# Earlier split of block 2's start, one run of matmuls for each neighbourhood row, and moved transpositions in the sticks and the sliding window

## The reference

```python
def second_block(x, ln_g, w_in, b_in, ...):
    hn = rms_norm(h, ln_g[l])
    proj = hn @ w_in[l] + b_in[l]
    glu_a, glu_b, z_conv, q, k, v, z_att = jnp.split(proj, cuts, axis=-1)
    y_conv = conformer_conv(glu_a, glu_b, dw_w[l], ...)
    y_att = neighbourhood_attention(q, k, v, rpb[l])
    ...
    h = h + y @ w_out[l]

def neighbourhood_attention(q, k, v, rpb):     # tokens as a grid with rows of 64
    def one_row(args):                         # each query row sees 8 key rows, 16 columns of each
        s = jnp.einsum("bhwd,bhiwjd->bhwij", q_row, k_win) * scale + bias
        p = jax.nn.softmax(s.reshape(B, N_HEADS, GRID_W, kh * KW), axis=-1)
        return jnp.einsum("bhwij,bhiwjd->bhwd", p, v_win)
```

## Time and profile before

| | |
|---|---|
| median of 3 runs | 2934.9 us (2932.89 to 2935.36) |
| the profiled execution, its own time | 2932.91 us |
| its span, first to last instruction | 2931.6 us |
| mean granted TensorE clock | 0.993 |
| TensorE busy | 2852.8 us (97%) |
| VectorE busy | 1929.8 us (66%) |
| ScalarE busy | 1306.0 us (45%) |

### The profile page before, as it was taken

One profiled execution on the slowest core, in us unless ns is written; L12 is line 12 of the kernel. 1 busy time (PEld: TensorE's weight loads), 2 busy tenths in 40 slices (PEclk: granted clock), 3 DMA queues, 4 the chain that ended last, 5 costly groups with the idle time before them and its releaser, 6 DMA issues.

```text
span 2931.6 us, 35692 instructions
## 1 busy us (share of the span) xinstructions
PE 2852.8 (97%) x14306; PEld 2222.7 (76%) x14306; DVE 1929.8 (66%) x2891; ACT 1306.0 (45%) x2069; POOL 13.3 (0%) x15
## 2 busy tenths in 40 slices
PE   8999999999999998999999999999899999999998
PEld 7887787788888886777775777666577788888886
DVE  5453439777777768776775685776767755555575
ACT  4223525434444346454545645556644433233335
POOL 0000000000000000000000000000000000000001
PEclk9999999999999999999999999999999999999999
DMA  4211111111111111111110110000001112111112
GB/s 161 78 57 40 40 51 37 52 49 58 44 58 58 44 58 51 37 36 37 36 36 22 43 51 22 23 23 30 30 30 51 44 43 65 51 47 55 58 51 79
DMA packets 49986, 141.73 MB, mean 48 GB/s; under 512 B 12918, under 2 KB 16798, under 8 KB 49694
## 3 DMA queue, kind: packets, MB, share of 16 engines
q1 hardware_dynamic: 49822, 139.45, 15.0%
HBM read 135.16 MB, written 9.77 MB: 49 GB/s over the span
## 4 chain that ended last, share of the span: by engine, by line
PE 80%; DVE 10%; ACT 5%; issue 4%; DMA 0%; POOL 0%; DVEq 0%; SPq 0%; ACTq 0%; POOLq 0%
PE psum L992 24%; PE psum L612 13%; PE psum L1070 13%; PE psum L1257 12%; PE psum L754 2%; PE psum L645 2%; PE psum L1382 1%; PE psum L1409 1%; PE psum L728 1%; PE psum L1198 1%; PE psum L685 1%; PE psum L1177 1%; PE psum L802 1%; DVE y L3247 1%; DVE mlp_ta L2930 1%
## 5 line engine op out<-in xcount | busy, mean ns | idle before, releaser
L2508 ACT ACTIVATE w_hi<-w_raw 128x512 fp32r<-128x512 f32 x280 | 175.1, 625 | 319.9 <-DVE w_raw L3831 190.8
L3105 DVE TENSOR_TENSOR residual<-residual,psum 128x1024 f32<-128x1024 f32 x160 | 194.3, 1220 | 122.5 <-PE psum L1070 122.4
L992 PE MATMUL psum<-h_hi,w_hi 128*128 128x512 f32 x640 | 249.1, 389 | 0.1
L992 PE MATMUL psum<-h_hi,w_lo 128*128 128x512 f32 x640 | 249.0, 389 | 0.0
L992 PE MATMUL psum<-h_lo,w_hi 128*128 128x512 f32 x640 | 249.0, 389 | 0.0
L3862 DVE TENSOR_TENSOR w_lo<-w_raw,w_hi 128x512 fp32r<-128x512 f32 x280 | 192.1, 686 | 36.0 <-ACT w_hi L2508 35.8
L612 PE MATMUL psum<-h_hi,w_hi 128*128 128x512 f32 x656 | 210.1, 401 | 4.1 <-DVE w_lo L2589 4.1
L1257 PE MATMUL psum<-h_hi,w_lo 128*128 128x512 f32 x608 | 209.9, 411 | 0.0
L1257 PE MATMUL psum<-h_hi,w_hi 128*128 128x512 f32 x608 | 206.8, 421 | 2.4 <-ACT cln_rstd L1481 1.4
L1070 PE MATMUL psum<-mlp_act_hi,w_hi 128*128 128x512 f32 x640 | 198.7, 392 | 6.1 <-DVE residual L3105 4.1
L612 PE MATMUL psum<-h_hi,w_lo 128*128 128x512 f32 x656 | 202.4, 390 | 0.0
(11 more groups left out here) (480 smaller groups left out, 5656.3 us busy)
## 6 DMA issues: line engine op xcount, KB each, us to landing
w_raw<-in_weights SPq DMA_DIRECT2D x228, 512.0 KB, 3.6
residual<-in_x_t SPq DMA_DIRECT2D x8, 512.0 KB, 8.5
out_t<-residual SPq DMA_DIRECT2D x16, 256.0 KB, 2.1
rel_copies<-rel_rows SPq DMA_DIRECT2D x8, 480.0 KB, 6.1
na_bias<-rel_copies SPq DMA_DIRECT2D x8, 240.0 KB, 4.5
band_copies<-band_rows SPq DMA_DIRECT2D x8, 192.0 KB, 6.0
ret_rotary<-in_rotary SPq DMA_DIRECT2D x1, 1024.0 KB, 12.0
swa_bias<-band_copies SPq DMA_DIRECT2D x4, 256.0 KB, 4.2
```

Source lines behind the costliest of these rows:

```text
L992: ins = self.pe.matmul(out[bank[j]], w[:, k, :], x(k), start=(j in emptied and k == 0 and part == 0), stop=(k == 3 and part == 2), skip_gr ...
L2508: ins = self.act.activation(dst, src, ACT.Copy)
L3105: self.dve.tensor_tensor(x, x, self.m.place["down", t, n], ALU.add).then_inc(*self.to("dve_down", t, n))
```

## The change

- **Block 2's start.** The squares of half 1 get places of their own in the idle tensor `y`, and VectorE's adds for that half go. TensorE makes their sum itself: `n4_squares` issues one fp32 matmul for each of the eight tiles, into the same bank, five ahead of the first projection and three at its tile (2, 0), where one stood. ScalarE makes the split of the first weight tile a square earlier, the root of half 0 two squares earlier, and the split of the second tile behind square 6 instead of behind all squares.
- **Neighbourhood.** The two runs of 9 are one of 18 (4 instead of 2 and 2 at the end); then come the products and then the turning. The orders of ScalarE and VectorE stay.
- **Sticks.** The run of 2 between scores and the first turning goes, and the run behind that turning is 6 instead of 4.
- **Sliding window.** The turning stands directly behind the scores, and one run of 8, 10 or 3 behind it.

```diff
     def n4_square(self, k, half):
+        if half:
+            return self.y[:, k // 2, k % 2 * HALF:k % 2 * HALF + HALF]
         return self.block_square(self.m_acc, (self.m_buf0, self.m_buf1), k, half)
...
+    def n4_squares(self, *tiles):
+        m = self.m
+        for k in tiles:
+            if k == 0:
+                self.n4_sum = self.take(("pe_n4_mean", 1), 5, 1, ("act_n4_rstd_ln", 1))
+            self.q.wait_ge(*self.on("act_n4_sq", k, 1))
+            ins = self.pe.matmul(self.n4_sum, m.c("mean1024"), m.n4_square(k, 1), start=(k == 0), stop=(k == KD - 1),
+                                 skip_group_check=True)
+        if tiles[-1] == KD - 1:
+            ins.then_inc(*self.to("pe_n4_mean", 1))
...
+        self.n4_squares(0, 1, 2, 3, 4)
         self.project_pair_halves(lambda k, half: ("act_n4_hi", k, half), lambda k, half: ("dve_n4_lo", k, half),
-                                 ("act_nq", 0), ("act_nv", 0), {(2, 0): lambda: self.n4_mean(1)})
+                                 ("act_nq", 0), ("act_nv", 0), {(2, 0): lambda: self.n4_squares(5, 6, 7)})
...
             if step < rows and r % 2 == 0:
                 self.na_scores(step)
-            self.run(rest, some)
+            self.run(rest, 2 * some)
             if p == PAIRS - 1 and 12 <= r < 16:
                 self.cln_square(r - 12)
+            if step >= 2:
+                self.na_out(step - 2)
             if 1 <= step <= rows:
                 self.na_turn(step - 1)
-            self.run(rest, some)
-            if step >= 2:
-                self.na_out(step - 2)
...
             self.stick_scores(d)
-            self.run(rest, 2)
             if d:
                 self.stick_turn(2 * d - 2)
-            self.run(rest, 4)
+            self.run(rest, 6)
...
-            filling = 4 if step < 6 else 5 if step < AHEAD else 3
-            if step != MEAN:
-                self.run(rest, filling)
             if TURN <= step < PAIRS * NCH + TURN:
                 self.window_turn(step - TURN)
-            if step < AHEAD:
-                self.run(rest, filling)
+            self.run(rest, 8 if step < 6 else 10 if step < AHEAD else 3)
...
# ScalarE, after_mlp1
-                before = squared_there(7 * half + k - 1 - 4) if k else None
-                if before:
-                    q.wait_ge(*on("dve_n4_acc", *before))
+                if k > 4 and half == 0:
+                    q.wait_ge(*on("dve_n4_acc", k - 4, 0))
...
-                if (half, k) == (1, 3):
+                if (half, k) == (1, 2):
                     self.split_up_to(B2)
-                elif (half, k) == (1, 5):
+                elif (half, k) == (1, 3):
                     self.n4_rstd(0)
+                elif (half, k) == (1, 6):
+                    self.split_up_to(B2 + 1)
...
     def norm4(self):
         m, q, on = self.m, self.q, self.on
-        self.split_up_to(B2 + 1)
...
# VectorE, after_mlp1
-                if k:
+                if k and half == 0:
                     waiting.append((k, half))
-        squared(*waiting.pop())
```

## The result

The changed kernel takes 2951.87 us in the median (four runs, 2947.88 to 2952.52), the kernel before 2933.89 in the same comparison: a ratio of 1.0063 with a 95% interval of 1.0051 to 1.0075, or 18 us more. The forecast was 2953, 17.8 more. The total is right; several of the terms behind it are not, and they cancel. So the total proves little, and the terms have to be read one by one.

A forecast was written before the change was run, and what follows sets the result against it. TensorE, busy for 97% of the span, was taken to bound the kernel. The terms summed to +17.8 us on the profiled 2932.9, so 2950.7; with 2.0 for the median the forecast was 2953, range 2939 to 2961.

The forecast's parts named there:

- B2, the boundaries: Neighbourhood, three pair boundaries: scores wait 3.35 us for queries evicted behind turning 14's copy, +8.1 us in all.
- B2, the clock: Neighbourhood, behind the three boundary waits: the granted clock falls, 1.5 us each, +4.5 us (0 to 9).
- The rival that the clock stays up: Pair boundaries: one wait of 3.35 us leaves the clock up, so without the 4.5, 2948 us; chance .22.
- B3: Neighbourhood, means of the squares at row 2, three pairs: each waits 1.65 us, +2.7 us (2 to 3.2).
- A: Start of block 2: root of half 1 starts only some 1.0 us sooner, −1.0 us (bounds −4 and +1).
- B1: Neighbourhood, order of a row: +.11 us for each of 28 pairs, less about .15 at six places, +2.1 us.
- C: Sticks: 47 steps lose one break (.09) and get a turning behind scores (.42 for .35), −1.4 us.
- D: Sliding window: earlier turning waits .9 and 1.2 us at steps 6 and 15, saved breaks return about .6, +1.5 us.
- B4: Last neighbourhood rows: ScalarE's last root, which the pointwise stage awaits, stands behind a later turning 62, +1.3 us.
- B5: Everything else on ScalarE in the neighbourhood: exponentials up to 3 us late cost nothing; 5 to 10 us if cover is gone.
- (5): Rival, faster: with (4), block 2's whole 9.0 us hole closes and the clock stays up, 2929 us; chance .06.
- (4): Rival, not slower: a turning costs .35 us wherever it stands, 2941.5 or 2937 us; chance .12.

The follow-up runs named there:

- the filling: Changed kernel with three fp32 matmuls of constants ahead of the wait for queries at the first scores of pairs 1 to 3: 2946.86 us, ratio 1.0046.
- eight ahead: Kernel before with only block 2's start changed, all eight squares of half 1 summed ahead of the projection: 2929.68 us, ratio .9989.
- the parts that paid: Kernel before plus eight squares ahead, sticks as changed, window as changed except steps 6, 15 and from 26 on: 2925.87 us, ratio .9975.
- the second kernel: Changed kernel with row 15 of the first three pairs and row 2 of pairs 1 to 3 in the old order: 2935.58 us, ratio 1.0005.

## Why the prediction was right

**B2, the boundaries: right, in mechanism and size.** A wait of 3.35 us was forecast from the chain turning, copy, queries, and 3.34 was measured three times; putting row 15 back took it away.

**B2, the clock: right in size, less certain than it was written.** 5.2 against 4.5, but as two stretches of 2.6 and one of none, and not three of 1.5. The rival that the clock stays up came true at one boundary of three, so the near sum is in part luck. And the longest wait that stood alone and left the clock up in the kernel before was 1.4 us, not 1.7: the one of 1.7 in the earlier trace rows came behind two of 1.2 and 1.3, and the clock was .50 from 2120.5 to 2127.3. The Trainium skill ("TensorE: Matmul & The Clock Gate", Part 1, What's actually happening) has the throttled state as the default that activity releases; the filling agrees: with 2.6 of the 3.34 idle us filled (.76 are left), .50 became 1.00.

**B3, the means: right as a wait** (1.63 against 1.65), incomplete as a price: in the kernel with row 15 put back each of these waits brought the clock down too, and undoing them gave 5.6 us and not 2.8. In the changed kernel and in that with the filled boundaries none of them did.

**A: the right term, and a bound that came true.** −1.0 was forecast, and the five other traces that hold this part as written show −1.0 to −1.2; in the changed kernel's own trace the bound of "+1 if the squares run at the low clock" held, with +.7. The step that named the three squares ahead of the root was right, as the kernel with eight ahead shows.

**B1: wrong by 2.5 us.** The failing step is the sum of prices of a pair of rows. The turnings cost what was forecast, .41 behind products and .59 ahead of scores. But the two long runs were charged .16 and .17 above 18 x .232, taken from runs of 9, and in the changed kernel they take .13 and .12 (4.31 and 4.30 us, medians over the plain pairs): a part of what a run of 9 takes above its matmuls goes with each break, and half of the breaks are gone. That is .08 a pair, 2.2 us in 28. A plain pair takes 11.86 us and took 11.87: no drift between boundaries and means. The prediction's other sum for this term was 0, from the Trainium skill (same page, Part 2, What happens when you issue a matmul), where matmuls keep their order and only weight loads are pulled ahead. That came closer, but not because a break is free: in a pair the runs lost .28 us with their breaks, and the turnings got .29 dearer.

**C: wrong by 2.1 us.** Over the 42 steps with nothing else in them a step takes 5.21 us and took 5.28 (means). The merged run saves .10, near the .09 charged. The failing step is the price of the moved turning, .42 for .35, that is .07 more, taken from other stages. In the sticks the scores and the first turning together got only .04 dearer, and the second turning, now behind a run of 6, got .02 cheaper, which the sum left out. The term should have been read from its own stage. The recorded sum is also off in itself: −.09 and +.07 are −.02 a step and −1 in all, not −1.4.

**D: wrong by 2.4 us.** Step 6 cost .9 as forecast. At step 15 the size of the wait was right (2.33 in place of .96, 1.4 more for 1.2), but the low clock behind it (1.5 us) was left out, although the same mechanism had been counted at the boundaries. The last .7 lies in the steps from 26 on, which the term left out too: the waits on ScalarE there are 1.9 us in five in place of .6 in two. The kernel with the parts that paid keeps the old order there and loses .2 there; no run changed these steps alone.

**B4** was +1.6 for +1.3, with the wait on `cln_rstd` at 2.5 for 1.4 as the step said, 1.1 longer. **B5** held: the waits on VectorE's maximum didn't grow, and the .4 us a mean in the second kernel is all that ScalarE's lateness cost in the ordinary rows.

One sum of the chances is off: the rest of (5) and half of (4) are .02 + .06 = .08 and not .10, which makes slower .88.

## What to carry to other kernels

A step that is moved behind others for the sake of a longer run has to be followed to the place where something waits for it: of the 56 rows ahead of the last eight, 50 didn't care, three cost 13 us and three some 3. Where a wait cannot be avoided, its price is the idle time and, where it falls, the clock behind it; matmuls of constants in the gap took the clock's part away here, but cost their own time where nothing was waited for. And take the price of an instruction from the stage in which it stands.

## What the runs showed that was not expected

The granted clock isn't settled by the length of a wait: idle times of 3.34 us brought it down twice and spared it once in one trace, and idle times of 1.63 brought it down at the three means of one kernel and at none of two others. At step 15 of the window a wait of 2.33 brought it down and one of 2.34 in another kernel did not. What decides between them no run here tells. What the stretch cost was steady, 2.5 to 2.7 us behind the boundaries and 1.5 to 1.7 behind the means and at step 15.
